# Two layers of a hybrid streaming encoder: the recurrent heads reordered as a software pipeline, with their roots taken on 12 columns

## What is computed

```python
def chunk_gated_delta(q, k, v, g, beta):
    ...
    decay = jnp.exp(jnp.where(causal, G[..., :, None] - G[..., None, :], -jnp.inf))
    kb = kc * bc[..., None]
    m = jnp.einsum('nbhid,nbhjd->nbhij', kb, kc) * decay
    m = jnp.where(idx[:, None] > idx[None, :], m, 0.0) + jnp.eye(CHUNK, dtype=m.dtype)
    sol = lax.linalg.triangular_solve(m, rhs, left_side=True, lower=True, unit_diagonal=True)
    qk = jnp.einsum('nbhid,nbhjd->nbhij', qc, kc) * decay
    def step(state, inp):
        v_new = u_i - jnp.einsum('bhck,bhkv->bhcv', w_i, state)
        o = jnp.einsum('bhck,bhkv->bhcv', qd, state) + jnp.einsum('bhij,bhjv->bhiv', qk_i, v_new)
        state = state * gl[..., None, None] + jnp.einsum('bhck,bhcv->bhkv', kd, v_new)
        return state, o

def gated_deltanet(q, k, v, z, b, a, conv_w, a_log, dt_bias, norm_w):
    qkv = jax.nn.silu(causal_dwconv(jnp.concatenate([q, k, v], axis=-1), conv_w))
    q = l2norm(q.reshape(b_, s_, DN_HEADS, DN_DK)) * (DN_DK ** -0.5)
    k = l2norm(k.reshape(b_, s_, DN_HEADS, DN_DK))
    ...
    o = (o * lax.rsqrt(jnp.mean(o * o, axis=-1, keepdims=True) + NORM_EPS)
         * norm_w.astype(f32) * jax.nn.silu(zf))
```

## Time and profile before

| | us |
|---|---|
| median of 3 runs (lowest to highest) | 3570.14 (3569.32 to 3572.62) |
| the profiled execution, device time | 3572.67 |
| its span | 3570.9 |
| PE busy (share of the span) | 3229.1 (90%) |
| DVE busy | 1632.5 (46%) |
| ACT busy | 749.2 (21%) |
| POOL busy | 1760.6 (49%) |
| mean granted TensorE clock | 0.946 |

### The profile page before, as it was taken

One profiled execution on the slowest core, in us unless ns is written; L12 is line 12 of the kernel. 1 busy time (PEld: TensorE's weight loads), 2 busy tenths in 40 slices (PEclk: granted clock), 3 DMA queues, 4 the chain that ended last, 5 costly groups with the idle time before them and its releaser, 6 DMA issues.

```text
span 3570.9 us, 41512 instructions
## 1 busy us (share of the span) xinstructions
PE 3229.1 (90%) x14312; PEld 2563.4 (72%) x14312; DVE 1632.5 (46%) x1994; ACT 749.2 (21%) x1313; POOL 1760.6 (49%) x1002
## 2 busy tenths in 40 slices
PE   7999998788868899999999999997888698999997
PEld 5888765567756777888778887556666577678885
DVE  3332455944453725332244325467554355253323
ACT  1110223321221222211021102232221212221101
POOL 5666432434314653766656664323333056556663
PEclk9999999899978999999999999998999799999998
DMA  3233211112102321333222332111111022223231
GB/s 132 94 100 100 86 65 42 53 54 65 42 30 71 101 89 54 103 97 99 96 84 94 96 104 86 48 54 54 54 48 59 12 95 83 89 77 100 94 100 53
DMA packets 78862, 272.59 MB, mean 76 GB/s; under 512 B 8176, under 2 KB 12560, under 8 KB 78736
## 3 DMA queue, kind: packets, MB, share of 16 engines
q1 hardware_dynamic: 73504, 264.27, 22.8%
q10 hardware_dynamic: 5088, 5.96, 0.5%
q0 software_dynamic: 144, 0.66, 0.0%
HBM read 268.73 MB, written 2.12 MB: 76 GB/s over the span
## 4 chain that ended last, share of the span: by engine, by line
PE 76%; DVE 12%; issue 6%; ACT 2%; POOL 2%; DMA 0%; DVEq 0%; POOLq 0%; ACTq 0%; SPq 0%
PE acc L460 65%; PE aux L460 9%; DVE dc L1425 1%; POOL wl L445 1%; DVE sq_sum L1327 1%; POOL wh L443 1%; DVE xl L1292 1%; ACT tmp L966 1%; DVE dc L1423 1%; DVE tmp L1623 1%; PE aux L623 1%; DVE tmp L1567 1%; DVE tmp L1570 1%; DVE dc L1563 0%; DVE tmp L1626 0%
## 5 line engine op out<-in xcount | busy, mean ns | idle before, releaser
L443 POOL TENSOR_SCALAR wh<-raw 128x1024 fp32r<-128x1024 f32 x496 | 536.7, 1082 | 1719.6 <-PE acc L460 964.4
L445 POOL TENSOR_TENSOR wl<-raw,wh 128x1024 fp32r<-128x1024 f32 x496 | 1224.7, 2469 | 41.4
L460 PE MATMUL acc<-xh,wh 128*128 128x512 f32 x2432 | 989.5, 407 | 70.9 <-POOL wl L445 37.2
L460 PE MATMUL acc<-xl,wh 128*128 128x512 f32 x2432 | 962.4, 396 | 0.0
L460 PE MATMUL acc<-xh,wl 128*128 128x512 f32 x2432 | 962.1, 396 | 0.0
L460 PEld LDWEIGHTS acc<-xh,wh 128*128 128x128 f32 x2432 | 464.9, 191 | 207.4 <-issue 70.0
L460 PEld LDWEIGHTS acc<-xh,wl 128*128 128x128 f32 x2432 | 465.5, 191 | 100.5
L460 PEld LDWEIGHTS acc<-xl,wh 128*128 128x128 f32 x2432 | 465.6, 191 | 94.7 <-issue 3.8
L460 PE MATMUL acc<-hh,wl 128*128 128x512 f32 x704 | 278.1, 395 | 0.0
L460 PE MATMUL acc<-hh,wh 128*128 128x512 f32 x704 | 278.1, 395 | 0.0
L460 PE MATMUL acc<-hl,wh 128*128 128x512 f32 x704 | 278.1, 395 | 0.0
(11 more groups left out here) (262 smaller groups left out, 4095.2 us busy)
## 6 DMA issues: line engine op xcount, KB each, us to landing
raw<-in_stream SPq DMA_DIRECT2D x496, 512.0 KB, 3.4
xf<-in_xT SPq DMA_DIRECT2D x1, 2048.0 KB, 10.0
bias<-rel_scratch ACTq DMA_DIRECT2D x2, 1024.0 KB, 5.5
mraw<-in_memT ACTq DMA_DIRECT2D x2, 1024.0 KB, 5.3
out_xT<-xf SPq DMA_DIRECT2D x1, 2048.0 KB, 7.1
gate_w<-in_gate_w ACTq DMA_DIRECT2D x2, 512.0 KB, 3.5
const<-in_const POOLq DMA_DIRECT2D x1, 640.0 KB, 8.0
sc<-in_ba_w ACTq DMA_DIRECT2D x2, 256.0 KB, 2.6
```

Source lines behind the costliest of these rows:

```text
L443: pool.tensor_scalar(wh[:, s, :], raw[:, s, :], 1.0, 0.0, ALU.mult, ALU.add).then_inc(hi_step, 1)
L445: pool.tensor_tensor(wl[:, s, :], raw[:, s, :], wh[:, s, :].bitcast(F32), ALU.subtract).then_inc(unit_split, 1)
L460: return pe.matmul(out, w, x, start=start, stop=stop, skip_group_check=True)
```

## The change

1. **A pipeline over heads.** The steps of a head are cut in three. While head h runs its levels, each level s also carries `beside(s, h + 1, h - 1)`: a piece of the next head's preparation and of the last head's output. The next head's k by k (`kk`) and transposed keys stand in the recurrence. A second `dc` and `hc` buffer hold the next head; `tt` moves from the decay tile to `tmp[3]`; the head's output goes to `li[:, h]`, its squares and z gate to `lr[:, h]`. The loop on head 0 is preceded by its own preparation, and the last head is followed by `delta_end`.
2. **Roots on 12 columns.** The sums of squares are one-column products (`columns`: `ones[:, 0:1]` or `rms_w` as the moving operand) that put a token on each partition: 4 columns for k, 4 for q, 4 for the last head's output, 12 in bank B5. One square root, one reciprocal of 128x12 (`rates`), and then `spread` turns each column of 4 back into 128x512 with products of a broadcast column and the identity. `decay_rows` is a product with a column of the identity; the step `g_row` goes.
3. **Order within a level.** `q` is issued before `qt`, and `n` is subtracted before `t`; the next level's `c` is taken right after `p`.
4. **Filler.** `FILL_LRU` is 12 for 8, so 28 parts have run before head 0; a head then takes 28 parts instead of 42, head 0's preparation 20 of its own, `delta_end` 4. The tile order changes with it (the z tile of head 1 comes first).

```diff
-    for m in range(4):
-        add("proj", 0, m)
-    for h in range(HN):
-        for d in (2 * h, 2 * h + 1):
...
+    heads(0, 0, 1, 2, 3)
+    heads(1, 3)
+    branches(0)
+    heads(1, 1, 0, 2)
+    branches(1)
+    branches(2)
+    heads(2, 1, 0, 2)
...
-FILL_LRU = 8
-FILL = {"sum_k": 9, "k_turned": 3, "inv0_turned": 6, "rms_sums": 2}
-FILL |= {f"p{s}": 2 for s in range(1, LEVELS)} | {f"qt{s}": 1 for s in range(1, LEVELS)}
-FILL |= {"w": 1, "v1": 1, "v2": 1, "v3": 1}
+FILL_LRU = 12
+FILL_AHEAD = {(0, "norm_cols"): 10, (0, "k_spread"): 4, (0, "q_spread"): 2, (0, "kk"): 2, (0, "k_turned"): 2,
+              (HN - 1, "rms_cols"): 2, (HN - 1, "o_spread"): 2}
+FILL = {"v_turned": 1, "kq": 1, "inv0_turned": 1, "w": 1}
+FILL |= {f"p{s}": 2 if 1 < s < LEVELS - 1 else 1 for s in range(1, LEVELS)}
+FILL |= {f"q{s}": 1 for s in range(1, LEVELS - 1)} | {f"qt{LEVELS - 1}": 1}
+FILL |= {f"{x}{c}": 1 for x in "vo" for c in range(CH)}
...
+def dve_beside(s, n, p):
+    return {1: only(n, "g_last", "decay_min", "kd_arg", "conv1"), 2: only(n, "decay", "silu1", "conv0"),
+            3: only(n, "silu0", "conv2"), 4: [(n - 1, "rate")], 5: only(n, "k_normed", "silu2") + only(p, "z_gate"),
+            6: only(p, "o_normed", "y") + only(n, "q_normed")}.get(s, [])
...
+                def columns(x, of):
+                    for c in range(CH):
+                        last = mm(B5[:, x * CH + c:x * CH + c + 1], of[:, c * P:(c + 1) * P], rms_w[:, :] if x == 2 else ones[:, 0:1])
+                    return last
...
+                def spread(n, x, step):
...
+                    for c in range(CH):
+                        last = mm(tiles(B5)[:, c, :], rates[:, x, c:c + 1].broadcast_to([P, P]), ident)
+                    done(last, n, step)
...
+                    if h + 1 < HN:
+                        dve(h + 1, "k_normed")
+                        keys_by_keys(h + 1)
...
-                    drain(l, filled_before(h, "rms_sums"))
-                    act_("rms_std")
-                    link(dve.reciprocal(tmp[1][:, :], tmp[1][:, :]))
-                    done(tt_(os_[:, :], os_[:, :], tmp[1][:, :], ALU.mult), "o_normed")
...
+                def inverse_roots(a, b, step):
+                    act_(step, "std")
+                    done(dve.reciprocal(rates[:, a:b, :], rates[:, a:b, :]), step, "rate")
```

More of the change, by code:

```diff
@@ L48 @@
 LRU_C = 8.0
-LAYER_LINKS = 209
+LAYER_LINKS = 197
 UNIT = 1024
@@ L77, in add, with branches, heads @@
         unit += ends
-    for m in range(4):
-        add("proj", 0, m)
-    for h in range(HN):
-        for d in (2 * h, 2 * h + 1):
-            add("gate", 1, d)
-            add("gate", 2, d)
-            add("up", 1, d, 0, ends=False)
-            add("up", 2, d, KB)
-        for m in range(4 if h < HN - 1 else 0):
-            add("proj", h + 1, m)
+    def branches(d):
+        add("gate", 1, d)
+        add("gate", 2, d)
+        add("up", 1, d, 0, ends=False)
+        add("up", 2, d, KB)
+    def heads(h, *parts):
+        for m in parts:
+            add("proj", h, m)
+    heads(0, 0, 1, 2, 3)
[5 more added lines that the diff above has]
+    heads(2, 1, 0, 2)
+    branches(3)
+    heads(2, 3)
+    heads(3, 1, 0, 2)
+    branches(4)
+    branches(5)
+    heads(3, 3)
+    branches(6)
+    branches(7)
     for d in range(0, KD, 2):
@@ L217, with delta_steps @@
[L217 to L221 removed]
+def delta_steps(ahead, beside, core, tail, end):
+    steps = [x for s in range(LEVELS) for x in beside(s, 0, -1)] + ahead(0)
+    for h in range(HN):
+        steps += core(h, lambda s: beside(s, h + 1, h - 1))
+        steps += tail(h, ahead(h + 1))
+    return steps + end(HN - 1)
@@ new lines, in keys_by_keys, with keys_turned @@
+                def keys_by_keys(n):
+                    filled(n, "kk")
+                    k = dc2[n % 2][:, 1, :]
+                    if n:
+                        act(n - 1, "w")
+                    for c in range(CH):
+                        tok = slice(c * P, (c + 1) * P)
+                        last = mm(tiles(B4)[:, c, :], k[:, tok], k[:, tok])
+                    done(last, n, "kk")
+                def keys_turned(n):
+                    filled(n, "k_turned")
+                    dve(n, "m")
+                    for c in range(CH):
+                        last = pe.transpose(tiles(B4)[:, c, :], dc2[n % 2][:, 1, c * P:(c + 1) * P], ident)
+                    done(last, n, "k_turned")
@@ L740, in delta @@
+                for s in range(LEVELS):
+                    beside(s, 0, -1)
+                keys_by_keys(0)
+                keys_turned(0)
+                for h in range(HN):
+                    dc, hc = dc2[h % 2], hc2[h % 2]
+                    filled(h, "v_turned")
+                    if h:
+                        dve(h - 1, "v3")
+                    dve(h, "silu2")
                     for c in range(CH):
                         last = pe.transpose(tiles(B6)[:, c, :], dc[:, 2, c * P:(c + 1) * P], ident)
-                    done(last, "v_turned")
@@ L757, in delta @@
-                    fill(l, FILL["inv0_turned"])
-                    dve("t0")
-                    act("kg")
-                    dve("kd")
+                    done(last, h, "v_turned")
+                    filled(h, "kq")
+                    if h:
+                        act(h - 1, "o_sq")
+                    dve(h, "q_normed")
+                    for c in range(CH):
+                        tok = slice(c * P, (c + 1) * P)
+                        last = mm(tiles(B5)[:, c, :], dc[:, 1, tok], dc[:, 0, tok])
@@ L775, in delta @@
+                        filled(h, f"q{s}" if s < LEVELS - 1 else f"qt{s}")
+                        act(h, f"p{s}")
                         if s == 1:
-                            act("vk")
-                            dve("qk")
-                        for c in range(CH):
-                            last = mm(tiles(B6)[:, c, :], tiles(tmp[2])[:, c, :], tt[:, c, :])
-                        done(last, f"qt{s}")
+                            act(h, "vk")
+                        else:
+                            dve(h, f"t{s - 1}")
@@ new lines, in keys_decayed, with level_0, keys_last @@
+                def keys_decayed(n):
+                    own(n, "decay")
+                    pe_(n, "kk")
+                    for c in range(CH):
+                        last = stt_(mt[:, c, :], tiles(B4)[:, c, :], cols[:, 1, c, n:n + 1], dt_[:, c, :], ALU.mult, ALU.mult)
+                    done(last, n, "m")
+                def level_0(n):
+                    own(n, "m")
+                    done(tt_(tiles(tmp[1]), mt[:, :, :], level_mask(0), ALU.mult), n, "c0")
+                def keys_last(n):
+                    act_(n, "kg")
+                    for c in range(CH):
+                        last = ts_(kd[:, c, :], tiles(B4)[:, c, :], hc2[n % 2][:, 1, c:c + 1], None, ALU.mult)
+                    done(last, n, "kd")
```

583 lines of the change are left out of this document (358 added, 225 removed).

## The result

| | before | after |
|---|---|---|
| median (lowest to highest), 4 runs each | 3569.73 (3568.57 to 3572.62) | 3391.29 (3390.21 to 3392.02) |
| ratio after / before, 95% interval | | 0.9496 (0.9485 to 0.9507) |
| span of the profiled execution | 3570.9 | 3390.2 |
| PE busy, share of the span | 3229.1 (90%) | 3187.3 (94%) |
| DVE busy | 1632.5 | 1561.4 |

Faster by 5.0%, 178 us; the forecast was 3387. The chain that ended last, by engine, answers to the earlier trace rows: TensorE's share rose, VectorE's fell by a third.

A forecast was written before the change was run, and what follows sets the result against it. TensorE's work and its waits were taken as the bound. Terms of 352.7 us a layer against 442.9 and 440.6, plus 2.4 a layer in branch A, saved 182.9 us: 3387 us forecast, own range 3350 to 3430, chance 0.58.

The forecast's parts named there:

- Filler and products: TensorE's work in a layer's heads: 140 filler parts at 1.37 us, 191.8 us, and the heads' products, 123.0 us.
- Levels 1 and 2: VectorE late with n because convolutions collide with GpSimd's subtractions: 1.0 us in each level, 2.0 a head, three heads.
- k by k: Next head's k by k waits for ScalarE's copy of w from the same bank: 1.1 us a head, three heads.
- Clock: TensorE's clock drops after waits in the overlapped heads: 0 to 1.7 us a head, 1.7 taken, three heads.
- Cold start: Low TensorE clock after the wait for the RG-LRU output at the start: 2.7 us a layer.
- Head 0's preparation: Before head 0's levels, its first sum waits for two convolutions beside GpSimd: 2.0 us a layer.
- The start: Before the heads, gate tiles ending 5.5 us later delay ScalarE's y_hi, moving VectorE's first y_lo by 2.0 us.
- (A): Rival: VectorE becomes the bound through the lock with GpSimd, 74 us, 84 with clock drops: 3471 us; chance 0.14.
- (B): Rival: TensorE's clock drops once for each level instead of once a head, 68 us more: 3455 us; chance 0.10.
- (C): Rival: nothing stalls in the new order, 20.4 us a layer less: 3346 us; chance 0.12.
- (D): Rival: the pipeline doesn't overlap and preparation stays on the path, 127 us more: 3514 us; chance 0.04.
- (E): Rival: slower, TensorE held at 1.2 GHz in the finely cut stage, up to 4017 us; chance 0.02.

The follow-up runs named there:

- p_nolock: Changed kernel with GpSimd's subtraction of a weight unit cut from 1024 to 256 columns, the rest of the low part left out: 3303.8 us, ratio 0.9255.
- p_dveorder: Changed kernel with VectorE's convolutions and silus behind each level's n and t, and head 0's third convolution behind the reciprocal: 3366.6 us, ratio 0.9420.
- p_order: Changed kernel with the old order inside a level, qt ahead of q and t ahead of n: 3395.2 us, ratio 0.9521.
- p_cols2: Changed kernel with every group of one-column sums issued twice: 3419.9 us, ratio 0.9586.
- p_split: Changed kernel with five filler parts moved within heads 0 to 2, between level 4's one-column sums and ahead of k by k: 3382.2 us, ratio 0.9460.
- p_wide: Changed kernel with unused 512-column reciprocals put back on VectorE before each narrow reciprocal: 3465.3 us, ratio 0.9703.
- p_yhi: Changed kernel with ScalarE writing y_hi before it evacuates the last of three filler tiles ahead of the heads: 3391.1 us, ratio 0.9483.
- p_best: Changed kernel with the edits of p_dveorder, p_yhi and p_split together: 3352.8 us, ratio 0.9379.
- s_roots: Kernel before, heads still serial, with only its roots taken on narrow columns: 3565.6 us, ratio 0.9983.

## Why the prediction was right, and where not

**The mechanism** was right: TensorE's work hardly changed, its waits went. The stretch was forecast at 352.7 - 14.75 = 338.0 us and took 335.0 and 334.7. Granted clock 0.98, no wide reciprocal, branch A at 0.39 us: as written. "No wait over 3 us" failed once a layer, in head 0's preparation, and the wait for the RG-LRU was 9.12 us, not 8.

**The terms.** Filler and products (191.8 + 123.0 = 314.8): the stretch less its idle time (14.3) and what its clock of 0.98 costs (about 2% of 335, 6.7) is 314.0. Only the sum is right for certain: counted from start to start, the filler took 203 us (1.45 a part, with its hand-overs, for 1.37) and the products 111, so the two terms were off by some 12 us each, in opposite directions. Table loads went from 16 to 12 a layer, one a head and not two; nothing was booked for them. The waits and the clock between them were booked at 23.1 (14.4 + 4.0 + 2.7 + 2.0) and came to 21.0, but by cancelling errors, which is luck:

- *Levels 1 and 2*, 6.0 booked, 6.8 found (1.31, 1.33, 1.33, and 2.83 in head 0's level 2 alone). Cause as argued, collisions with GpSimd (p_nolock), where the convolution stands ahead of n (p_dveorder). In head 0's level 2 an `up` tile's evacuation stands there as well, 0.68 and 2.14 us (L1738, L1742), behind the convolution and ahead of n.
- *k by k*, 1.1 a head booked, 0.69 found.
- *Clock*, 1.7 a head booked, for falls behind short waits. Waits of 1.3 us brought none, and the 2.83 us wait none in this execution. But the mechanism and its price are real: behind waits of 1.9 us in p_order and behind six of ten of 2.8 us the clock did fall, mostly for 3.4 us, which is 1.7 lost. In the changed kernel there was one fall a layer, half of some 3.4 us, behind the narrow sums, a cause that I had not seen (p_cols2, p_split). I had priced those at their passes alone.
- *Small waits*, 4.0 booked, 0.8 found. *Cold start*, 2.7 booked; the clock was back 3.2 us after the wait in layer 0, 1.6 lost, and 5.6 us after it in layer 1, 2.8 lost.
- *Head 0's preparation*, 2.0 booked: the step that failed most. It waited 4.66 us and ran at 0.50 for another 5.3, 7.3 in all (5.9 in layer 1). The text let "its first sum" wait for two convolutions; the sums did not wait. What waited was all that stands behind them: TensorE's queue waits for the narrow reciprocal before the four parts of filler and the spread of k, and on VectorE that reciprocal stands behind the third convolution and an `up` tile's evacuation. The timeline of DVE there:

```profile
689.51 2.58 DVE L1631 TENSOR_SCALAR dc<-dx,par 128x512 f32<-128x512 f32 x1
692.13 2.32 DVE L1633 SCALAR_TENSOR_TENSOR dc<-dx,par,dc 128x511 f32<-128x511 f32 x3
694.37 0.68 DVE L1736 SCALAR_TENSOR_TENSOR xf<-gt,acc 128x512 f32<-128x512 f32 x1
694.97 0.68 DVE L1738 SCALAR_TENSOR_TENSOR gt<-gt,acc 128x512 f32<-128x512 f32 x1
695.68 0.69 DVE L1742 TENSOR_TENSOR xf<-xf,gt 128x512 f32<-128x512 f32 x1
696.29 0.19 DVE L1777 RECIPROCAL rates<-rates 128x8 f32<-128x8 f32 x1
```

  The expectation of p_dveorder named the filler tile's bank instead. That is excluded by p_wide, where reciprocals put between the evacuation and the narrow one lengthen the wait to 11.13 us. p_dveorder moved the convolution behind the reciprocal, and 0.59 us remained. Whether the four parts of filler, put ahead of that wait, would cover it was not run.
- *The start*, 2.0 booked, 2.7 found (VectorE's gate product of this stage stands 3.58 us later than before, the wait's end 6.32). The size was right by luck and the cause wrong: not ScalarE's queue (p_yhi), but VectorE, 2.20 + 0.66 us longer beside the additional split on GpSimd. No run takes that one split away alone.

**The rivals.** (A), the lock as the bound, had the mechanism and the wrong size: the trace shows the product of 2.88 us and first taps of 2.61, and the shorter subtraction is worth 11.5 us a layer, where (A) asked for 42. The Trainium skill's rule (SBUF — State Buffer, section "Who interferes with whom") that the loser is blocked for the whole instruction agrees with those rows. What (A) had wrong is less VectorE's loss (35.7 us in layer 0's stretch, for 7 x 2.2 x 3 = 46) than that it reaches TensorE: the idle time there is 14.5 us, all causes together. (B), a swinging clock, did not come, but its kind of loss is real, by another way in. The Trainium skill (TensorE: Matmul & The Clock Gate, section "A second HAM failure mode: psum-queue depth-cycling") names frequent micro-idles; here the clock fell behind sums with no idle time at all, and behind single waits of 1.9 to 2.8 us. (C), nothing stalls, is nearly what p_best is, though not the kernel that was forecast: 318.9 against 317.6 for the stretch without those terms. (D) and (E) are excluded by a head of 73.4 us and a clock of 0.98.

**What I expected of s_roots** was wrong by a factor of ten, because the work that narrow roots add to TensorE was not subtracted, and the prediction would have failed on a change that had made the roots alone.

## What to carry to other kernels

When one engine bounds a stage, count what it waits for, spread the independent work evenly over those waits, and move the other engines' work beside it; here the even filler was worth 28 us a layer and the pipeline 70. Then look at the order on the engine that has become nearly full: put what the bounding engine needs next ahead of the long operations that nobody needs yet (10 us a layer for no work saved). Cheaper operations on a side engine, bought with work on the bounding one, may be worth nothing until the schedule needs their room, and much once it does. And take a stretch apart into idle time, time at half clock and work before naming a cause: the same 3.4 us can be any of them.
